# The turned attention output of the first block moves out of a weight slot, and the streamed expert weights take their slots in another order

## The reference, cut to what matters

```python
z = h @ w_in                                  # 1024 x 5128
o_a = from_heads(fox_attention(fq, fk, fv, log_f))          # 8 heads of 64
a = (p1 - lam * p2)                                         # 4 "diff" heads, two softmaxes each
ob = rms_norm(a @ v, g_subln) * (1.0 - lam_init)
y = gate_a * (o_a @ w_pa) + gate_b * (o_b @ w_pb)
x = x + y @ w_o
...
gl = hf @ w_group + b_group                   # 4 groups of 8 experts, top 2 within the best group
yb = (silu(xblk @ w1[e]) * (xblk @ w3[e])) @ w2[e]          # 32 experts, 1024 -> 512 -> 1024
x = x + out
...
proj = h @ w_in_2                             # second block, 1024 x 10240
```

## Time and profile before

| | |
|---|---|
| three timed runs | 1044.08, 1045.11, 1045.23 us (median 1045.11) |
| profiled execution, its own time | 1041.2 us |
| its span from first to last instruction | 1039.4 us |
| mean granted TensorE clock | 0.983 |
| PE busy | 993.1 us, 96% of the span |
| DVE, ACT, POOL busy | 391.2, 375.6, 123.7 us |
| DMA | 307.95 MB, mean 296 GB/s |

### The profile page before, as it was taken

The page is one execution under the profiler, slowest core; times in us unless marked ns, Lnnn a source line. Parts: engine busy times, 40 slices in busy tenths (PEclk is TensorE's granted clock), DMA queues, the critical chain, the costliest instruction groups (busy, mean ns, idle before and its releaser), DMA issues.

```text
span 1039.4 us, 14926 instructions
## 1 busy us (share of the span) xinstructions
PE 993.1 (96%) x6369; PEld 698.2 (67%) x6369; DVE 391.2 (38%) x749; ACT 375.6 (36%) x611; POOL 123.7 (12%) x82
## 2 busy tenths in 40 slices
PE   7999999999999999979999999988999999999996
PEld 7887788975444444333443444348989999999994
DVE  4456356853121211121121211126334444773564
ACT  4546656541211111101111112225445555554442
POOL 2110111020000000000000000002321111441122
PEclk9999999999999999989999999998999999999999
DMA  8974494399999999999999999996545544445301
GB/s 270 372 275 163 136 339 174 131 418 416 422 422 422 420 421 421 420 420 421 420 421 421 421 421 421 421 400 244 198 166 185 186 170 163 163 167 208 133 1 41
DMA packets 84038, 307.95 MB, mean 296 GB/s; under 512 B 6609, under 2 KB 13170, under 8 KB 59386
## 3 DMA queue, kind: packets, MB, share of 16 engines
q1 hardware_dynamic: 80178, 302.16, 74.1%
q10 hardware_dynamic: 3784, 4.73, 1.5%
HBM read 305.82 MB, written 2.63 MB: 297 GB/s over the span
## 4 chain that ended last, share of the span: by engine, by line
PE 76%; DVE 9%; ACT 4%; SPq 4%; DMA 3%; issue 2%; POOL 1%; POOLq 0%; DVEq 0%; ACTq 0%
PE bank L778 74%; SPq L834 4%; DMA ring<-in_w 3%; DVE arena L1284 3%; DVE arena L1281 2%; DVE wR L1278 2%; DVE arena L1278 1%; ACT arena L2028 1%; PE bank L1231 1%; ACT wR L1851 1%; DMA arena<-in_rows 1%; PE bank L972 1%; POOL wR L2222 1%; ACT arena L1913 0%; DVE small L1281 0%
## 5 line engine op out<-in xcount | busy, mean ns | idle before, releaser
L778 PE MATMUL bank<-hTR,wR 128*128 128x256 f32 x2520 | 315.9, 286 | 5.4 <-DVE hTR L1278 2.3
L778 PEld LDWEIGHTS bank<-hTR,wR 128*128 128x128 f32 x2520 | 307.5, 193 | 9.9 <-issue 5.0
L778 PE MATMUL bank<-ring,arena 128*64 128x512 f32 (+2 forms) x1056 | 228.6, 602 | 8.4 <-issue 6.7
L1851 ACT ACTIVATE wR<-ring 128x1024 fp32r<-128x1024 f32 x161 | 168.3, 1054 | 106.7 <-PE bank L778 104.9
L1278 DVE TENSOR_TENSOR wR<-ring,wR 128x1024 fp32r<-128x1024 f32 x125 | 155.8, 1250 | 132.4 <-ACT wR L1851 132.1
L778 PE MATMUL bank<-arena 128*64 128x512 f32 (+7 forms) x778 | 164.5, 529 | 0.7 <-DVE small L1410 0.7
L778 PEld LDWEIGHTS bank<-ring,arena 128*64 128x64 f32 (+2 forms) x1056 | 70.1, 136 | 141.2 <-issue 137.4
L1284 DVE SCALAR_TENSOR_TENSOR arena<-bank,small,arena 128x256 f32<-128x256 f32 x32 | 15.5, 484 | 346.3 <-ACT arena L2028 346.3
L1999 ACT ACTIVATE arena<-bank,small 64x512 f32<-64x512 f32 x62 | 42.3, 683 | 280.6 <-PE bank L778 280.3
L2222 POOL TENSOR_TENSOR wR<-ring,wR 128x1024 fp32r<-128x1024 f32 x36 | 87.9, 2441 | 311.1 <-ACT wR L1851 311.1
L778 PEld LDWEIGHTS bank<-arena 128*64 128x64 f32 (+4 forms) x778 | 63.5, 148 | 83.7 <-issue 77.1
(11 more groups left out here) (208 smaller groups left out, 835.0 us busy)
## 6 DMA issues: line engine op xcount, KB each, us to landing
ring<-in_w SPq DMA_DIRECT2D x120, 1024.0 KB, 20.6
arena<-in_w SPq DMA_DIRECT2D x72, 1024.0 KB, 20.0
ring<-in_w_in SPq DMA_DIRECT2D x29, 2048.0 KB, 8.7
ring<-in_w_ada SPq DMA_DIRECT2D x6, 2048.0 KB, 8.0
ring<-in_w_o SPq DMA_DIRECT2D x2, 2048.0 KB, 11.6
ring<-in_w_o_attn SPq DMA_DIRECT2D x2, 2048.0 KB, 7.9
ring<-in_w_o_conv SPq DMA_DIRECT2D x2, 2048.0 KB, 8.6
ring<-in_w_out SPq DMA_DIRECT2D x2, 2048.0 KB, 8.0
```

What stands on the lines that cost most here:

```text
L778: return pe.e.matmul(o, l, r, start=start, stop=stop)
L1851: eng.activation(h, w, ACT.Copy).then_inc(s_high, 1)
```

## The change

The buffers YT move from 89 and 91 KB to 8 and 10 KB of the arena, onto the first half of `hTR` (the normed, turned input, whose last readers are the gate tiles). The first chunk in slot 6 no longer waits for `s_y` but for the matmuls of `diff_out` 3 and the turn of `diff_turn` 2. The order of the eight slots was 5, 6, 1, 2, 7, 3, 4, 0 and is 6, 1, 5, 2, 3, 7, 4, 0; the five of the second block keep their order 1, 2, 3, 4, 0. In turn i = 8 of the attention loop one call of `next(fill)` is left out, so that the filling work from there on comes one call later: what stood at the first place of turn 8 stands at the second, what stood at the second stands at the first of turn 9, and so on to the last call of turn 15, which found the generator empty before.

```diff
-        YT = [area(89, 512), area(91, 512)]
+        YT = [area(8, 512), area(10, 512)]
...
-        turn8 = [RING, RING + 1] + [(n_first + i) % RING for i in range(2)] + [RING + 2]
-        turn8 += [(n_first + i) % RING for i in range(2, RING)]
+        next5 = [(n_first + i) % RING for i in range(RING)]
+        turn8 = [RING + 1, next5[0], RING, next5[1], next5[2], RING + 2, next5[3], next5[4]]
...
-            if i > 7 or i % 2:
+            if i > 8 or i % 2:
                 next(fill, None)
...
-                elif slot_of[nm] in (RING, RING + 1):
+                elif slot_of[nm] == RING:
                     e.wait_ge(s_y, 4)
+                elif slot_of[nm] == RING + 1:
+                    filled(e, U_["do", 3])
+                    filled(e, U_["dt", 2])
```

## The result

The changed kernel takes 1039.76 us (median of 18 runs, 1037.75 to 1043.60), the kernel before 1044.61 us (18 runs beside them, 1042.83 to 1047.12). The medians differ by 4.85 us; the measured ratio is 0.9961, with a 95% interval of 0.9952 to 0.9970, which is 4.1 us less, between 3.1 and 5.0. The forecast was 3.5 us less, 1041.6.

The account below looks back on a forecast made before the run. PE was taken as the bound, nearly balanced with the expert weight stream. Removed idleness 2.04 plus slow matmuls 1.57 gave 3.6, rounded to 3.5 us: 1045.1 - 3.5 = 1041.6; own range 1040.9 to 1042.6, 8-in-10 range 1039.4 to 1045.6.

Parts of the forecast that it names:

- The early slot: Before the expert weight stream: c0 and c1 load sooner, up to 10 us moved forward, but by itself worth 0.
- the 1.73 us of the rival: Expert stream: c8 and c9 keep their lead, PE's two late waits for weights go too; 1039.9, chance 0.10.
- the hole stretches: Weight stream between 216 and 255 us, where the 10 us of two chunks moved forward would be lost again.
- the filling order: Attention from turn 8: filling work one call later brings attention steps sooner, removing 2.04 us idleness and perhaps 1.57 us.
- The chain: Attention steps feeding p_turn 11: soft 13 starts at 152.1, diff_mix 3 ends at 174.1, 1.6 us before PE arrives.
- the slower rival: Between soft 15 and diff_mix 3, one more DVE split of 1.22 us delays p_turn 11; 1046.3, chance 0.09.
- the long L1281: DVE instruction in diff_mix 2, 2.10 us beside POOL's split; expected back at 0.23 us, saving 1.87 us.
- The lock that spoke against the change: DVE and GpSimd's shared SBUF ports: DVE's next split loses at most 0.9 us; in full, 0.3 us idleness stays.
- The sum: At p_turn 11: PE's work before it unchanged, reached at 175.7; gain 2.04 us idleness plus 1.57 us slow matmuls.
- the clock's term: Tile behind p_turn 11: 4.62 - 3.05 = 1.57 us of slow matmuls, gone if the clock fell for the idleness.
- The first rival: At p_turn 11 the idle time goes but the slow clock doesn't; gain 2.0 or 1.0 to 2.0, 1043.3, chance 0.15.
- A sign that was off: Expert stream: c10 would be issued about 3.5 us sooner than 255.69.

## Why the prediction was right or wrong

**The early slot is worth nothing: right, and shown.** Alone it is 0.9995 (0.9986 to 1.0004), which excludes the 1.73 us of the rival, and taken away it leaves 0.9957. The reason was c10, pinned to PE's reading of c2. The column "turn to c10" is that pin. The rates in the hole stretches show where its 10 us went.

**The gain comes from the filling order: right, and shown.** 0.9967 (0.9954 to 0.9979) with that one line.

**The chain: right in its places.** Soft 13 was put at 152.1 and came at 151.9 (on the clock of the profile before), the end of diff_mix 3 at 174.1 and came at 178.7 - 4.28 = 174.4. Soft 15 came 4.4 us sooner (170.61 - 4.28 against 170.75), where 4 was said, which put the slower rival out. The relief from the long L1281 came as priced. The lock that spoke against the change did come back, on DVE's split of the next piece, 1.95 us in place of 1.23: 0.7 us, under the 0.9 allowed. By the Trainium skill, SBUF — State Buffer, section "Who interferes with whom", a DVE instruction with two SBUF inputs contends with a GpSimd instruction that reads SBUF; the trace agrees, with those numbers.

**p_turn 11 was reached sooner than said.** The sum held PE's work up to there unchanged, 175.7; it came at 179.47 - 4.28 = 175.2. So 2.57 us were won between p_turn 6 and 11, of which 2.04 are the idleness; the other 0.5 lies in PE's row itself. From start to start, 0.16 of it is at the waiting place too, because the modelled end of diff_turn's matmuls counts there as busy. 0.13 lies in the two halves of the ada product, now neighbours, which take 3.57 us and took 1.85 twice, and the rest in pieces of 0.14 and less where other kinds of matmul follow one another. I put this down to the neighbourhood by the rows; no run isolates it.

**The step that was mis-sized is the clock's term.** The sum had "2.04 + 1.57 = 3.6 us", the second for the slow tile. The slow tile was real in the one profile and is no steady part: with the same idleness it is missing in two other profiles, and filling the idleness showed no gain in the timed runs, 0.9999 and 1.0005. The first rival said this and had 0.15. Even where the slow tile was paid, it cost 1.0 us at the router and not 1.57. What was set against it, that PE's row had no gap and the clock no dip between 14 and 175 us, misread the row. It has idle times of 1.07, 0.71 and 0.73 us; the last two:

```profile
60.47 3.10 PE L778 MATMUL bank<-hTR,wR 128*128 128x256 f32 x24 [0.71 <-POOL wR L2222]
...
73.86 1.13 PE L778 MATMUL bank<-arena 8*128 8x256 f32 x4 [0.73 <-DVE small L1410]
```

They were not followed by a slow clock in this execution. In 10 of the 14 profiles used here the clock did fall behind the last of them, between 74 and 84 us. So the profile before already held short waits that cost no clock, which spoke for the rival. In place of 2.04 + 1.57 stand 2.57 between the two turns and 0.05 from there to the router: 2.6 us, in each pair of profiles whose clock did not fall behind p_turn 11, and 3.6 against the one where it did. The total of the forecast, 3.5, is close to the measured 4.1 (3.1 to 5.0) partly by luck.

**A sign that was off.** c10 was to come 3.5 us sooner. On the clock of the profile before it came at 257.81 - 4.28 = 253.5, 2.2 us sooner, as the clock fell in the routing for 6.8 us in this execution and for 3.4 in the one before.

**What stays open.** 2.6 us of shorter work are 0.25%; the four timed kernels with the new filling order and no fillers (0.9961, 0.9967, 0.9957, 0.9965) say 3.4 to 4.5 us. The rest, about 1 us, may be the clock: from the router to c10 the distance is 25.98, 27.3 or 28.7 us, as the clock falls there for none, 3.4 or 6.8 us, and p_turn 6 comes between 118.7 and 123.1 us, in large part in the same way. The mean granted clocks of the timed runs point that way: 0.9847 over the 66 runs of the kernel before and 0.9847 over 34 of edited kernels with the old filling order, 0.9860 over 73 with the new one, with standard errors of 0.0002 to 0.0004. As an estimate, 0.0013 x 1042 us is 1.4 us of work at most. It is an upper bound: behind c10 the profiles of the table have between 14 and 22 us of slow clock, and the distance to the end does not follow it. So the runs with the new order met less slow clock on average; how much of the 1 us that is, no run shows. That the early slot adds half a us is not excluded either (0.9986 to 1.0004 alone).

## What to carry to other kernels

Before an earlier buffer is credited with time, find the first transfer whose slot is freed by the consumer itself, and compare its issue with what an unbroken stream would want; if it is already late, nothing ahead of it counts. When one late operand stalls the bound engine, follow its chain through the other engines' queues: a queue entry that waits for something else, or a neighbour's lock, is often what makes it late, and moving one independent piece of work can be enough. Price a slow clock behind a stall from more than one execution, and look in the profile for other short stalls that cost no clock.

## What the runs showed of the hardware that was not expected

Where the granted clock can fall is much the same in every profile here; whether it falls there is not, and that makes some us per execution. Behind the one idle time of 5.9 to 6.3 us on PE, near 460 us, it fell in all 14 profiles; between 74 and 84 us, behind 0.73 us of idleness, in 10; in the routing in 11. The same program with the same 2.04 us of idleness had a tile of 4.62 us behind it in one profile and of 3.11 in the next. In the routing, a stretch thin in matmuls, the same work from router to c10 took 25.98 us with the clock at 2.4 GHz throughout (granted clock 1.00 from 229 to 245 us), and 28.7 when it spent 6.8 us at 1.2 GHz (0.79 over these 16 us). The Trainium skill, TensorE: Matmul & The Clock Gate, section "What's actually happening", says that the monitor's windows run free of the kernel; the runs agree in that equal gaps are not charged equally.

A matmul of 128x128 in float32 on the identity took 0.234 us here at the full clock, two records of 0.117 each: 15 calls are a row of 30 records and 3.51 us. A row of the profile counts records, not calls, and that made the fillers seem half as long as they are.
